# A two-layer transformer kernel: the memory's tiles, the last softmax inverse and the first output chunk in another order

## The reference

```python
def hybrid_mixer(h, w_in, b_forget, conv_w, conv_b, conv_ln_g, conv_ln_b, w_out):
    ...
    u = a * jax.nn.sigmoid(g)
    u = causal_depthwise_conv(u, conv_w, conv_b)
    u = jax.nn.silu(layer_norm(u, conv_ln_g, conv_ln_b))
    ...
    att = forgetting_attention(q.reshape(shp), k.reshape(shp), v.reshape(shp), log_f)
    att = att.reshape(B, S, FOX_WIDTH)
    return jnp.concatenate([u, att], axis=-1) @ w_out
...
        mem_n = rms_norm(mem, norm_memkv[l])
        y = memory_cross_attention(h, mem_n, w_mq[l], w_mk[l], w_mv[l], w_mo[l])
```

## Time and profile before

| | |
|---|---|
| median of 3 runs | 2246.6 us (2245.58 to 2247.1) |
| the profiled execution | 2249.11 us, span of its instructions 2247.2 us |
| mean granted TensorE clock | 0.955 of full |
| PE busy | 2119.4 us (94%) |
| weight loads (PEld) busy | 1731.7 us (77%) |
| VectorE (DVE) busy | 1322.2 us (59%) |
| ACT busy | 837.6 us (37%) |
| GpSimd (POOL) busy | 936.5 us (42%) |

### The profile page before, as it was taken

How to read it: one execution, slowest core, us unless ns; L and a number is a source line. 1 busy time by engine, 2 the same in 40 slices (tenths; PEclk the granted TensorE clock), 3 DMA queues, 4 the chain that set the end, 5 groups by cost and what they waited for, 6 DMA issues and landing times.

```text
span 2247.2 us, 23701 instructions
## 1 busy us (share of the span) xinstructions
PE 2119.4 (94%) x9729; PEld 1731.7 (77%) x9729; DVE 1322.2 (59%) x1665; ACT 837.6 (37%) x1209; POOL 936.5 (42%) x401
## 2 busy tenths in 40 slices
PE   8999989889999998999999999999988799999997
PEld 5677768767888887787877877878877687887786
DVE  7665871635234543465377776455677837777653
ACT  4623455552122224566243333333321324333322
POOL 4352135544444445112434444453676443444443
PEclk9998879989999998999999999989999989999998
DMA  6322112211222221111212223214231221232221
GB/s 208 137 87 75 38 38 79 90 56 67 103 94 94 94 94 54 41 49 56 76 57 94 96 94 110 94 57 178 94 141 52 98 76 59 99 104 95 95 94 38
DMA packets 34560, 194.05 MB, mean 86 GB/s; under 512 B 3903, under 2 KB 4495, under 8 KB 14932
## 3 DMA queue, kind: packets, MB, share of 16 engines
q1 hardware_dynamic: 34452, 192.54, 24.5%
HBM read 178.82 MB, written 13.64 MB: 86 GB/s over the span
## 4 chain that ended last, share of the span: by engine, by line
PE 61%; DVE 24%; ACT 9%; POOL 3%; issue 2%; DMA 0%; ACTq 0%; SPq 0%; DVEq 0%; POOLq 0%
PE ps L133 55%; DVE TMP L162 9%; DVE TMP L168 6%; PE ps L132 5%; ACT WH L149 4%; POOL X L156 1%; ACT TMP L150 1%; DVE TMP L156 1%; ACT PAD L149 1%; PE ps L141 1%; DVE ps L168 1%; DVE Y L156 1%; DVE X L156 1%; DVE VG L156 1%; DVE X L168 1%
## 5 line engine op out<-in xcount | busy, mean ns | idle before, releaser
L156 POOL TENSOR_TENSOR WL<-W,WH 128x2048 fp32r<-128x2048 f32 (+3 forms) x156 | 667.6, 4281 | 1012.9 <-ACT WH L149 1012.9
L133 PE MATMUL ps<-HH,WL 128*128 128x512 f32 (+1 forms) x1408 | 556.5, 395 | 29.9 <-DVE HL L168 8.1
L133 PE MATMUL ps<-HL,WH 128*128 128x512 f32 (+1 forms) x1408 | 546.0, 388 | 0.0
L133 PE MATMUL ps<-HH,WH 128*128 128x512 f32 (+1 forms) x1408 | 545.9, 388 | 0.0
L149 ACT ACTIVATE WH<-W 128x2048 fp32r<-128x2048 f32 (+2 forms) x150 | 278.5, 1857 | 321.3 <-PE ps L133 321.3
L133 PEld LDWEIGHTS ps<-HH,WL 128*128 128x128 f32 x1408 | 270.4, 192 | 101.5 <-issue 34.8
L133 PEld LDWEIGHTS ps<-HH,WH 128*128 128x128 f32 x1408 | 269.5, 191 | 53.9
L133 PEld LDWEIGHTS ps<-HL,WH 128*128 128x128 f32 x1408 | 270.3, 192 | 50.4 <-issue 0.2
L156 DVE TENSOR_TENSOR MRL<-MID,MRH 128x512 fp32r<-128x512 f32 x76 | 177.4, 2366 | 162.4 <-ACT MRH L149 162.4
L162 DVE TENSOR_SCALAR TMP<-PAD,PAR 128x512 f32<-128x512 f32 x88 | 208.9, 2374 | 76.3 <-ACT PAD L149 76.3
L133 PE MATMUL ps<-MRH,WL 128*128 128x512 f32 x608 | 238.4, 392 | 4.5 <-DVE TMP L168 2.2
(11 more groups left out here) (355 smaller groups left out, 3377.2 us busy)
## 6 DMA issues: line engine op xcount, KB each, us to landing
W<-in_up SPq DMA_DIRECT2D x44, 1024.0 KB, 4.8
W<-in_down SPq DMA_DIRECT2D x22, 1024.0 KB, 4.8
W<-in_w_up SPq DMA_DIRECT2D x16, 1024.0 KB, 4.8
W<-in_w_down SPq DMA_DIRECT2D x16, 1024.0 KB, 4.8
W<-in_hy_in SPq DMA_DIRECT2D x12, 1024.0 KB, 4.8
kd<-STG SPq DMA_DIRECT2D x36, 256.0 KB, 2.0
KB<-kd SPq DMA_DIRECT2D x8, 1024.0 KB, 5.0
W<-in_win_ag SPq DMA_DIRECT2D x4, 1024.0 KB, 4.8
```

The source lines that it names most:

```text
L133: return self.eng.matmul(out, lhs, rhs, start=start, stop=stop)
L156: return QUIET if self.eng is None else self.eng.tensor_tensor(out, a, b, op)
```

## The change

Three things are moved; no instruction is added or left out.

- VectorE makes memory tiles 0 and 1 ahead of the inverse of head 7's sums, tiles 2 and 3 right behind it, and tiles 4 to 7 behind the low part of head 6, all ahead of the scaling of the convolution's four tiles (before: all eight behind that scaling).
- ACT copies the first output chunk behind gated tile 1 instead of behind the four gated tiles and key tiles 0 and 1; VectorE makes its half of the low part behind its low part of gated tile 1.
- Head 7's high and low parts come ahead of those of key tiles 0 and 1.

```diff
 scalar_program
                         high(HH[:, j, :], CO[:, j, :], ("cat", j))
+                        if j == 1:
+                            weights(CH["w_out"][0])
+                    fox_high(7)
                     mem_k_high(0)
-                    weights(CH["w_out"][0])
-                    fox_high(7)
 vector_program
+            def scaled_memory(first, last):
+                for k in range(first, last + 1):
+                    dve.wait_ge(*at("mrs"))
+                    vacant("mn", k)
+                    dve.stt(tmp("mn", k)[:, 0:256], MX[:, k, :], par("g_memkv", k), RS[:, 0:256], ALU.mult,
+                            ALU.mult).then_inc(*out(("mnt", k)))
...
                     if h == 6:
                         inverse(("cq2",), 16, [("col", "crs")])
+                        scaled_memory(0, 1)
                     convolve(3, 3)
                     fox_rcp(h + 1)
+                    if h == 6:
+                        scaled_memory(2, 3)
                 convolve(7, 3)
                 if h == 7:
                     for j in range(4):
                         low(HL[:, j, :], CO[:, j, :], HH[:, j, :], ("cat", j))
+                        if j == 1:
+                            weights(CH["w_out"][0])
+                fox_low(h)
+                if h == 7:
                     mem_k_low(0)
-                    weights(CH["w_out"][0])
-                fox_low(h)
                 qk_out(h + 4)
...
                 if h == 6:
+                    scaled_memory(4, 7)
                     dve.wait_ge(*at("crs"))
                     for j in range(4):
                         dve.tt(CO[:, j, :], CO[:, j, :], bank("crs")[:], ALU.mult).then_inc(
                             *out(("xn_", j), *[("free", "crs")] * (j == 3)))
-                    dve.wait_ge(*at("mrs"))
-                    for k in range(8):
-                        vacant("mn", k)
-                        dve.stt(tmp("mn", k)[:, 0:256], MX[:, k, :], par("g_memkv", k), RS[:, 0:256], ALU.mult,
-                                ALU.mult).then_inc(*out(("mnt", k)))
```

## The result

The changed kernel takes 2239.19 us in the median of 6 runs (2235.32 to 2242.19), the kernel before 2246.85 us in the 6 runs beside it (2244.88 to 2248.12). The ratio is 0.9968 with a 95% interval of 0.9955 to 0.9980: 4.5 to 10.1 us faster, clear of noise. The question for the experiments was therefore where 2 us more than forecast came from (7.2 by the ratio, 7.7 between the medians, against 5.4).

The account below looks back on a forecast made before the run. PE was taken to bind the kernel except where it stands still; 4.0 us from the first hole plus 1.4 from the second make 5.4, taking the runs' median of 2246.6 to 2241.2 us, range 2240.0 to 2244.3.

Parts of the forecast that it names:

- both holes: PE's idle time before the output projection: 4.47 us ahead of the memory's keys, 1.36 us waiting for the first output chunk.
- Step 1: Tiles 0 and 1 (0.79 us) fit VectorE's 0.76 us wait before the last softmax inverse; inverse moves 0.03 us, taken as 0.
- Step 2: ACT rounds the first memory tile at 327.11 instead of 330.65, 3.5 us earlier; GpSimd starts at 327.6.
- Step 3: GpSimd's eight lows take 6.3 us (bounds 5.6 and 6.8) instead of 6.80, ending at 333.9, a gain of 4.0 us.
- Step 4: PE still needs 11.21 us from GpSimd's last low to the keys' end, now 345.1; VectorE's operand part early by 1.3.
- Step 5: First output chunk copied by ACT at 337.75, ready at 343.1, 2.0 us before PE asks; the 1.36 us wait disappears.
- Steps 6 and 7: Keys' copies behind the last head cost nothing; second output chunk ready at 353.5, asked for at 356.0, slack 2.5 us.
- this rival: PE's clock falls in the middle of the keys, costing 1.5 to 3.4 us: 2242.7 to 2244.6; chance 0.20.
- The half clock throughout: Half clock for all 11.2 us of dense work behind GpSimd: net 5.8 us slower, 2252.4; chance 0.04.
- the chunk as the wait: ACT's chunk copy over 2.0 us late, PE waits up to 1.4 us again: 2241.3 to 2242.7; chance 0.08.
- the lost gain: Second chunk or a later copy binds behind the projection's start, 2 to 5 us lost: 2243 to 2246.6; chance 0.08.

Follow-up runs that it names:

- padded kernel: 7 extra matmuls of 256 columns, their result overwritten, ahead of the last key tile, against the kernel before: 2246.88 us against 2245.31 (ratio 1.0004).
- two halves of the change: Against the kernel before: only the memory's tiles moved, 2241.68 us (ratio 0.9986); only the first output chunk's copy moved, 2244.22 us (ratio 0.9997).
- tiles alone: Only the memory's tiles moved on VectorE, ACT's and VectorE's order at h = 7 as before, against the kernel before: 2241.68 us against 2245.31 (ratio 0.9986).
- keys side by side: Changed kernel with key tiles 0 and 1 made in one loop over the memory's tiles, chunk's copy still behind gated tile 1: 2242.24 us, one run.
- four tiles ahead: Changed kernel with all four first memory tiles ahead of the last softmax inverse instead of two: 2242.67 us, one run.
- 50 extra matmuls: Changed kernel with 50 overwritten matmuls of 256 columns ahead of the last key tile: 2245.50 us against 2245.31 for the kernel before (ratio 0.9996).
- chunk alone: Only the first output chunk's copy moved behind gated tile 1, memory tiles as before, against the kernel before: 2244.22 us against 2245.31 (ratio 0.9997).
- second profile of the kernel before: The kernel before, unaltered, profiled again: 2247.88 us, one run; stage 26.29 us.
- first comparison: Changed kernel against the kernel before, 6 runs each: 2239.19 us against 2246.85 (ratio 0.9968).
- in the second: The changed kernel again, unaltered, beside more runs of the kernel before: 2239.44 us against 2246.76 (ratio 0.9974).
- the keys side by side and the chunk behind tile 0: Changed kernel with key tiles 0 and 1 in one loop and the first chunk's copy behind gated tile 0: 2237.15 us against 2246.76 before (ratio 0.9959).

## Why the prediction was right or wrong

**What bounds the kernel.** Right: both holes were real. The padded kernel showed the second (about 1.7 us of delay for 0.21), the two halves of the change showed each alone.

**Step 1, the inverse.** Right. It comes 0.23 us behind the last exponential (324.18 against 323.95); before, 0.22. Its cover is as thin as said: two tiles fit, four cost 0.7.

**Step 2, the first low.** Predicted 3.5 us earlier; 3.6, measured from the last exponential (3.23 against 6.86).

**Step 3, eight lows.** Predicted 6.3 us with bounds of 5.6 and 6.8; the row has 6.31. The split is right too, not only the sum: the lows start 0.68 to 0.73 us apart where no tile of VectorE meets them and 0.87 to 0.88 apart beside tiles 4 to 7. GpSimd ends 4.1 us earlier (9.54 us behind the exponential against 13.66), 4.0 predicted.

**Step 4, the keys.** From the product with the eighth tile to the projection 10.97 us (333.55 to 344.52), 11.15 before. PTL ended at 335.43, 1.4 us ahead of its use.

**Step 5, the chunk.** Copy at 337.27, halves ended at 342.71 (339.25 + 3.46), 1.8 us before PE asked (2.0 predicted). The two late gated tiles waited for GpSimd's half on VectorE, as said (3.29 us for two lows), and held nobody.

**Steps 6 and 7.** The second chunk's low half ended at 353.10 (348.50 + 4.60), ahead of its use 10.9 us behind 344.52. The first 44.4 us behind the projection's start are of equal length before and after, with PE busy throughout at clock 1.00; beyond that no wait was compared one by one.

**The sum.** 5.4 predicted, 5.66 measured: the first hole gave 4.14 (4.0), the second 1.53 (1.36).

**The rivals.** The clock stayed at 1.00 from the first key matmul to the projection in all three profiles of the changed kernel, and in those of the tiles alone and of the keys side by side. In two kernels of nearly its order it fell there (four tiles ahead, 50 extra matmuls), early enough to cost 0.2 us, where 1.5 to 3.4 had been priced. The rule of the Trainium skill, "TensorE: Matmul & The Clock Gate", "HAM oscillation — how this bites in real kernels", by which bursts of matmuls with waits between them bring back the half clock, is told there of waits far longer than those between the paced matmuls here (0.26 us), so it speaks less for this rival than the prediction took it to; with these short waits two kernels lost the full clock and four profiles (the three of the changed kernel, the tiles alone) kept it. A wait as long as the page's stood only in the old order (4.47 us), and there the trace agrees: the clock fell in it in all four profiles. The prediction read from one profile that before the change the full clock is back just when the dense part begins. That was in part luck of the profile: it held with the chunk alone too, but in the second profile of the kernel before the full clock came 0.6 us later and cost 0.35 us, in the padded one 2 us later and cost 0.9. The rival was at work in the old order, hidden under the wait for the chunk. The half clock throughout, the chunk as the wait and the lost gain didn't come.

**What failed** is one term of the range: "down to 2240.0 (all lows at 0.70, and half a microsecond of scatter)". No row stands behind the 0.5 us, and the prediction had two in hand against it: the profiled execution lay 2.5 us above the median of the runs, and its own sentence that a measurement of this kernel can't tell 4.5 us from no change. The 35 runs of the unaltered kernel beside the halves lie between 2241.87 and 2251.80 with a standard deviation of 2.9 us; medians of six drawn from them lie within 1.6 us of the middle two times in three (an estimate from these runs). With 2 us for scatter the range would have been about 2238.5 to 2246 and would have held the 2239.19. The chance of "faster by over 0.2%" would have been lower than 0.61, since the forecast lay only 0.9 us beyond that mark.

**What stays open** is the 1.5 to 2 us that the first comparison has on top of the stage. The stage gives 5.66 of it in profiles that repeat. In whole runs, the gain by the ratio less what the stage gives is 1.5 us in the first comparison, 0.2 in the second, 1.4 with 50 extra matmuls, 1.4 with the keys side by side and the chunk behind tile 0, and -1.0, -0.9 and -0.7 for the two halves and the 7 extra matmuls, each with an interval of 2 to 3 us either way. Scatter alone can make these. But the four with a plus are the kernels that hold the whole change, and some of them share their runs of the kernel before, so a standing gain of about 1 us behind the stage isn't excluded.

## What to carry to other kernels

Find the place where the bounding engine stands still, name for each such hole the one instruction that ends it, and follow that instruction back over the other queues to the work that stands in front of it without need: here a scaling that nobody wanted for 9 us, and a weight chunk's copy behind four tiles that it didn't depend on. Moving work under a wait of another engine is free only up to the length of that wait (0.76 us held two tiles, not four). And measure a stage between two of its own events in one profile: that repeated to 0.06 us, where whole executions of this kernel, at 2.9 us of standard deviation, need dozens of runs to tell 2 us (an estimate). Then look inside the stage as well: a wait at its end can hide what happened ahead of it, as the wait for the chunk did in the kernel before.

## What the runs showed of the hardware that wasn't expected

The same code behind the projection took from 1889.3 to 1898.0 us in twelve profiles, and the code ahead of the stage from 323.36 to 326.61, in a program on one core. In one stretch of 502 matmuls it was 125.8 to 132.5 us in five of them, with TensorE's half clock (1.2 GHz) at other places of the same work each time. What decides where it falls was not tried.

The order VectorE and GpSimd take turns in also showed where it wasn't asked for: two of VectorE's lows with both inputs in SBUF, 0.69 us each alone, took 3.29 us together behind GpSimd's half of the chunk, while its low that reads PSUM kept its 0.69 us beside one in the kernel before.
